# Where the last chunk's residual sum lives, and new offsets and transfer times for the planner that orders a whole transformer block

## The reference, cut to what matters

```python
h = rmsnorm(x, g_mix)
z = h @ w_in                                  # 1024 -> 5120
bc, cc, vc, q, k, va, gc_pre, ga_pre = split(z)
g_c, g_a = sigmoid(gc_pre + b0), sigmoid(ga_pre + b1)
y_c = (bc * causal_dwconv3(cc * vc)) @ w_conv_out
q, k = rope(rmsnorm(q)), rope(rmsnorm(k))     # 4 heads, two sub-heads of 64 each
w = softmax(q0 k0') - lam * softmax(q1 k1')   # lam = exp(..) - exp(..) + lam_init
y_a = (rmsnorm(w @ va) * (1 - lam_init)) @ w_attn_out
x = x + (g_c * y_c + g_a * y_a) @ w_o         # the mix and the residual sum
gt, up = split(rmsnorm(x, g_ffn) @ w_gate_up) # 1024 -> 2 x 2816
x = x + (silu(gt) * up) @ w_down              # 2816 -> 1024
```

## Time and profile before

| | us |
|---|---|
| median of 3 runs (lowest) | 2353.46 (2350.31) |
| the profiled execution | 2351.96 |
| its span, slowest core | 2350.1 |
| spans of its 8 cores | 2330.6 to 2350.1 |
| TensorE busy in that span | 2201.4 (94%) |
| VectorE, ScalarE, GpSimd busy | 1076.7, 1074.0, 478.2 |

### The profile page before, as it was taken

How to read it: one execution, slowest core, us unless ns; L and a number is a source line. 1 busy time by engine, 2 the same in 40 slices (tenths; PEclk the granted TensorE clock), 3 DMA queues, 4 the chain that set the end, 5 groups by cost and what they waited for, 6 DMA issues and landing times.

```text
span 2350.1 us, 45681 instructions; the slowest of 8 cores (2330.6 to 2350.1 us)
## 1 busy us (share of the span) xinstructions
PE 2201.4 (94%) x14976; PEld 1134.7 (48%) x14976; DVE 1076.7 (46%) x2590; ACT 1074.0 (46%) x2011; POOL 478.2 (20%) x797
## 2 busy tenths in 40 slices
PE   5878999999899899999999999999989999999699
PEld 2333454454345444555445554455544555554344
DVE  6875446455443356434554245532435423343432
ACT  4542364363336433466345664456653566641010
POOL 2122335313330124200341003410023200010000
PEclk9998999999999999999999999999999999999899
...
GB/s 198 207 165 162 146 181 161 165 185 182 202 186 193 204 205 167 124 126 169 180 146 128 134 186 140 145 116 136 179 110 144 117 113 141 161 91 175 227 143 175
DMA packets 137031, 376.97 MB, mean 160 GB/s; under 512 B 13536, under 2 KB 34400, under 8 KB 136672
## 3 DMA queue, kind: packets, MB, share of 16 engines
...
## 4 chain that ended last, share of the span: by engine, by line
PE 75%; DMA 12%; issue 5%; DVE 4%; POOL 2%; ACT 2%; SPq 0%; DVEq 0%; POOLq 0%; ACTq 0%
PE bank L788 46%; PE bank L1225 12%; PE bank L1079 10%; PE bank L1053 6%; DMA wP<-wsc 3%; DMA kT<-wblk 2%; DMA xr<-xT 1%; DMA wsc<-wM 1%; DMA xs<-x 1%; DMA wP<-wblk 1%; DMA out<-xr 1%; DMA wM<-wblk 1%; DMA csj<-css 1%; DVE scrM L1148 0%; DMA css<-big 0%
## 5 line engine op out<-in xcount | busy, mean ns | idle before, releaser
L1064 ACT ACTIVATE Pb<-bank 128x512 bf16<-128x512 f32 (+1 forms) x1088 | 557.7, 590 | 271.0 <-PE bank L1053 268.5
L788 PE MATMUL bank<-h,wM 128*128 128x512 bf16 x2720 | 635.7, 383 | 9.1 <-DVE h L1192 8.2
L788 PEld LDWEIGHTS bank<-h,wM 128*128 128x128 bf16 x2720 | 259.0, 98 | 308.8 <-issue 31.4
L788 PE MATMUL bank<-h,wP 128*128 128x512 bf16 x1584 | 380.0, 382 | 11.1 <-DMA wP<-wsc 6.9
L1079 PEld LDWEIGHTS bank<-Vs,Pb 128*128 128x128 bf16 x4224 | 274.8, 99 | 114.6 <-issue 25.8
L1079 PE MATMUL bank<-Vs,Pb 128*128 128x129 bf16 x4224 | 321.8, 221 | 3.3 <-ACT Pb L1064 1.4
L1225 PE MATMUL bank<-big,wM 128*128 128x512 bf16 x1344 | 316.5, 381 | 2.9 <-DMA wM<-wblk 2.9
L788 PEld LDWEIGHTS bank<-h,wP 128*128 128x128 bf16 x1584 | 148.6, 98 | 185.9 <-issue 30.4
L1204 ACT ACTIVATE scrM<-bank 128x512 f32<-128x512 f32 x176 | 105.2, 597 | 287.7 <-PE bank L788 283.9
L1206 DVE SCALAR_TENSOR_TENSOR scrM<-scrM,bank 128x512 f32<-128x512 f32 x176 | 120.6, 685 | 194.6 <-ACT scrM L1204 176.5
L788 PE MATMUL bank<-wP,h 128*128 128x512 bf16 x720 | 175.3, 389 | 21.8 <-DMA wP<-wsc 9.1
...
## 6 DMA issues: line engine op xcount, KB each, us to landing
...
x1s<-big SPq DMA_DIRECT2D x64, 256.0 KB, 5.6
xr<-x1s SPq DMA_DIRECT2D x64, 256.0 KB, 4.5
out<-xr SPq DMA_DIRECT2D x64, 256.0 KB, 3.1
xr<-xT SPq DMA_DIRECT2D x56, 256.0 KB, 4.8
```

The costliest lines, as they stand in the source:

```text
L788: ins = nc.tensor.matmul(out(), lhsT=lhs(k), rhs=rhs(k), start=(k == first), stop=(k == last))
L1064: pl.op("act", lambda P=P, n=n, N=N, s=st[p, n]: nc.scalar.activation(out=Pb[:, P.slot[1], n, 0:N], in_=bk(s)[:, 0:N], func=AF.Exp, scale= ...
```

## The change

Five edits. (1) For the last chunk (j = 7) the residual sum no longer lies in `big`: four of its tiles lie in `h1` and four in the tiles of `scrP`, its `xT` is loaded straight into them, and its AO and WO weights go through `wP` instead of `wM`. A key `x1free` orders these loads behind the eight AO products, which are themselves ordered behind the last reader of `h1`. (2) `PERT` has 24 offsets, one for each stage of each chunk, which shift the priorities of TensorE. (3) Three constants of the model for transfers: those of the first 4 us of the plan are taken as 1.5 times as long and 0.7 us later, and later ones that meet traffic of the other queue as 1.3 us later (`BOTH`). (4) The exponential for `lam` and the two operations behind it wait for the fourth tile of `h1`, not for the first. (5) The scratch tiles of mix 7 have a sequence of their own (`M7`). Edits 2 and 3 change no instruction, only the order.

```diff
-EARLY = 1.0
+EARLY = 1.5
+BOTH = 1300.0
...
-PERT = {}
+PERT = {("A", 0): -0.218, ("A", 1): 0.407, ("A", 2): -0.074, ("A", 3): 0.02, ("A", 4): 0.074, ("A", 5): 0.082, ("A",
+        6): -0.277, ("A", 7): -0.15, ("M", 0): 0.151, ("M", 1): -0.269, ("M", 2): -0.16, ("M", 3): -0.24, ("M", 4): -0.309,
...
+TAILX = True
...
-                b = max(start + DMA_LAT, ring[q])
+                b = max(start + DMA_LAT + (700.0 if start < 4000.0 else 0.0), ring[q])
...
-                fin = ring[q] + 700.0
+                fin = ring[q] + 700.0 + (BOTH if over > 0.0 and start > 4000.0 else 0.0)
...
         def later_trig():
+            pl.op("act", lambda: nc.scalar.activation(out=small[:, SM_E + 2:SM_E + 4], in_=small[:, SM_E:SM_E + 2], func=AF.Exp),
+                  ["sm_e", ("h1", 3)], ["sm_e2"], 200)
...
-        pl.op("act", lambda: nc.scalar.activation(out=small[:, SM_E + 2:SM_E + 4], in_=small[:, SM_E:SM_E + 2], func=AF.Exp),
-              ["sm_e", ("h1", 0)], ["sm_e2"], 200)
...
-            name = "wP" if b < H_AO else "wM"
+            name = "wP" if b < (H_GU if j == NST - 1 and TAILX else H_AO) else "wM"
...
         def mix(j, fp):
+            tail = j == NST - 1 and TAILX
+            spare = [pl.tile("scrP", "P") for _ in range(4)] if tail else []
+
+            def xv(dc):
+
+                if not tail:
+                    return x1[:, dc, :]
+                if dc < 4:
+                    return h1[:, 2 * dc:2 * dc + 2, :].rearrange("p a b -> p (a b)").bitcast(F32)
+                return p_(spare[dc - 4])[:, 0:T]
...
+            free = [("h1", t) for t in range(4)] + ["x1free"] if tail else []
+            need = ["x1free"] if tail else []
...
-                    range(4), 0, 3, lambda part, hh=hh, dc=dc: [hh, ("gateA", dc), ("mixT", dc)] + [("onT", j % NON, k) for k in part], [b], PM)
-                m2 = pl.tile("scrM", "M")
+                    range(4), 0, 3, lambda part, hh=hh, dc=dc: [hh, ("gateA", dc), ("mixT", dc)] + [("onT", j % NON, k) for k in part], [b] + free, PM)
+                m2 = pl.tile("scrM", "M7" if tail else "M")
...
+                if tail:
+                    pl.dma("sp", lambda dc=dc: nc.sync.dma_start(out=xv(dc), in_=xT_d[dc * 128:(dc + 1) * 128, j * T:(j + 1) * T]),
+                           need, xk(dc), ("x0", dc), 262144, 1)
...
-                    out=x1[:, dc, :], in0=bk(b)[:], scalar=0.5, in1=xr[:, xt.slot[1], :] if xt else x1[:, dc, :], op0=ALU.mult, op1=ALU.add),
-                    [b] + ([xt] if xt else x1k(dc)), x1k(dc), DS512)
+                    out=xv(dc), in0=bk(b)[:], scalar=0.5, in1=xr[:, xt.slot[1], :] if xt else xv(dc), op0=ALU.mult, op1=ALU.add),
+                    [b] + need + ([xt] if xt else xk(dc)), xk(dc), DS512)
```

More of the change, by code:

```diff
@@ L1137, in mix, with xk @@
         def mix(j, fp):
+            tail = j == NST - 1 and TAILX
[6 more added lines that the diff above has]
+                return p_(spare[dc - 4])[:, 0:T]
+            def xk(dc):
+                return x1k(dc) if not tail else [("h1x", dc)] if dc < 4 else [spare[dc - 4]]
+            free = [("h1", t) for t in range(4)] + ["x1free"] if tail else []
+            need = ["x1free"] if tail else []
             if j == 0 and X0P:
@@ L1155, in mix @@
                 xt = None
-                if j > 0 or not X0P:
+                if tail:
+                    pl.dma("sp", lambda dc=dc: nc.sync.dma_start(out=xv(dc), in_=xT_d[dc * 128:(dc + 1) * 128, j * T:(j + 1) * T]),
+                           need, xk(dc), ("x0", dc), 262144, 1)
+                elif j > 0 or not X0P:
                     xt = pl.tile("xr", "M")
                     pl.dma("sp", lambda xt=xt, dc=dc: nc.sync.dma_start(
-                        out=xr[:, xt.slot[1], :], in_=xT_d[dc * 128:(dc + 1) * 128, j * T:(j + 1) * T]), [], [xt], ("xr", xt), 262144, 1)
+                        out=xr[:, xt.slot[1], :], in_=xT_d[dc * 128:(dc + 1) * 128, j * T:(j + 1) * T]), need, [xt], ("xr", xt), 262144, 1)
                 b = pl.tile(fp, "M")
@@ L1192, in mix @@
                 pl.op("dve", lambda R=R, dc=dc: nc.vector.scalar_tensor_tensor(
-                    out=h2[:, dc, :], in0=x1[:, dc, :], scalar=cst[:, C_GFFN + dc:C_GFFN + dc + 1], in1=bk(R)[:], op0=ALU.mult,
-                    op1=ALU.mult), x1k(dc) + [R, "cst"], [("h2", dc)], DS512)
+                    out=h2[:, dc, :], in0=xv(dc), scalar=cst[:, C_GFFN + dc:C_GFFN + dc + 1], in1=bk(R)[:], op0=ALU.mult,
+                    op1=ALU.mult), xk(dc) + [R, "cst"], [("h2", dc)], DS512)
         def ffn(j, fp):
```

22 lines of the change are left out of this document (11 added, 11 removed), and 2 rows, old and new, of the table PERT.

## The result

The changed kernel takes 2323.61 us (median of 4 runs, 2313.46 to 2350.89) beside 2351.89 us for the kernel before on the same chip. The ratio is 0.9868, 95% interval 0.9819 to 0.9917. Forecast were 2321 us in a range of 2294 to 2344. One run of each kernel, 2350.89 us of the changed one, was disturbed, and the ratio leaves both out.

The account below looks back on a forecast made before the run. The prediction took TensorE's own work as the bound. Its terms summed as 2351.96 - 19 - 5 + 0 - 8 = 2320 us for the profiled execution, forecast as a 2321 us median, range 2294 to 2344.

Parts of the forecast that it names:

- The last mix: Mix of the last chunk: weaving it with chunk 6's GU removes TensorE's 21.0 us loss, less new waits; -19 us.
- rival (d): Last chunk: the edit does not act, the `x1free` wait costs TensorE 10 us or more; at least 2331 us, chance 0.09.
- The boundary: Where chunk 0 ends: `tabs` operations behind the last head spare it VectorE's wait for `csj`, AO earlier; -5 us.
- The start: First microseconds: moved exponential and new early constants gain nothing, since the weight casts cover it; 0 us, -1.3 to +1.
- The middle: Between 215 and 2189 us: half of the 17.0 us of waits for projection weights goes; -8 us, -25 to +14.
- (b): Rival: the gain stays at the end, only the last mix and the boundary count; 2329 us, chance 0.19.
- (a): Rival: the whole weave improves, the middle giving 25 us and the boundary 9.2; 2299 us, chance 0.24.
- (c): Rival: the changed weave in chunks 4 to 6 is slower, `wP` and `wM` loads holding each other up; 2370 us, chance 0.06.

Follow-up runs that it names:

- tail_m7: tail_plain plus one offset of -0.5 for the last chunk's mix and feed-forward part; 0.9917 of the kernel before.
- tail_plain: Kernel before with only the last chunk's new buffers, its weights through `wP` and the scratch tiles' own sequence, no offsets, old constants; 0.9976 of the kernel before.
- m7_start_exp: tail_m7 with the new constants for the first 4 us and the moved exponential; 0.9886 of the kernel before.
- no_refit: Changed kernel with the old transfer constants, all 24 offsets and the moved exponential kept; 0.9943 of the kernel before.
- exp_back: Changed kernel with the exponential back in its old place, ahead of the first normalised input; 0.9885 of the kernel before.
- no_pert: Changed kernel with only the offset of the last chunk's mix, the 23 others taken out; 0.9863 of the kernel before, 0.9877 when run again.
- np_csj_early: no_pert with chunk 1's eight `tabs` operations moved on VectorE's list ahead of the last steps of chunk 0's last head; 0.9891 of the kernel before.

## Why the prediction was right, and where it wasn't

The forecast was 2321 us, measured were 2323.6 and, by the later ratio, 29.0 us less than before where 32 (1.4%) were forecast. The number came out for the last mix and the boundary, and in part by luck for the rest. By its steps:

**The last mix, -19 (-21 to -13).** Right in size: 19.6 us by tail_m7; taking the buffers out costs 21 to 25, at or beyond the end of the range. The gap-free TensorE from 2100 us on and the clock of 1.00 are as named, but for one wait of 1.42 us, for a load of `wM`, some 80 us behind the `xT` loads. The load of `wM` behind them was costed at nothing. The new waits were taken as 1.5 + 0.5 = 2.0 us and came to 0 and 0.19: the first `xT` load landed in at most 4.3 us, not 7.1, and VectorE stood 1.20 us instead of up to 3.6, behind which TensorE shows no wait. The row used is a median of seven loads, and what counts here is the first of eight. The DMA issues of the changed kernel from 2100 to 2130 us (KB each, median us to landing):

```profile
h<-xT SPq DMA_DIRECT2D x4, 256.0 KB, 5.1
scrP<-xT SPq DMA_DIRECT2D x4, 256.0 KB, 7.0
```

The first four took 5.1 us in the median, the next four 7.0, close to the 7.1 of the earlier trace rows. The rule of the Trainium skill, "DMA: Bandwidth & Descriptors", section "Anatomy of one DMA", which by estimate gives 2.6 us for 256 KB, was too short here (the section gives it for transfers that GpSimd issues, and these are issued by SP), and the row of before too long for the load that counts. By either, TensorE's wait would have been small. The place of the 9.25 us was read rightly and their cause only by half: in tail_plain the waits of VectorE for `xr<-xT` in the midst of WO are gone with the new buffers alone, which gave 5.7 us of whole time; the weave gives the other 13.9. That the edit doesn't act, rival (d), falls: TensorE waited 0 us for the `x1free` chain.

**The boundary, -5 (-9.2 to 0).** Right, in mechanism and size. AO was foretold at about 139.5 and began at 138.5 on the slowest core, and at 138.0 and 140.3 on the means of two executions, from 144.4. The experiments with eight moved operations give 7.3 and 7.6 us at AO, 5.1 and 5.2 a chunk later, and 3.3 to 6.6 in whole times, which the intervals don't tell from 0 by themselves. `csj` was in time behind the head.

**The start, 0 (-1.3 to +1).** Not contradicted for the exponential, open for the constants. Without the exponential ahead the first TensorE instruction comes 1.5 us earlier, and 0.2 of them are left at AO of chunk 0, which one execution of each can't tell from 2. m7_start_exp, which has both start edits, was 7.3 us faster than tail_m7, outside this range if it holds, at the very edge of its interval. And no_refit, with no table load ahead but the old constants, has its first TensorE instruction at 15.3 us, so the constants move it as well. The rule of "ScalarE: Activation LUTs", section "What ACT_TABLE_LOAD costs", in the Trainium skill would have 2.66 us in place of 1.28; here the next activation began 1.29 us after the load did, with no pause ahead of the load either (9.18 us, where the instruction before it ended at 9.16). TensorE's shift of 1.5 us decides nothing between them, since two loads stand ahead in exp_back.

**The middle, -8 (-25 to +14).** Too large, and for the wrong reason. The term was half of the 17.0 us that TensorE waits for `wP<-wsc`. These waits were 17.6 us after the change, where some 8 were foretold. Idle time between 220 and 2100 us fell from 68.4 to 63.6 and 67.6 us on the cores' mean, 1 to 5 us. The whole gain less the other terms leaves 29.0 - 19.6 - 5 = 4 us, by subtraction. The 23 offsets, which were the largest part of the edits it was to come from, are worth 0 within 6 us; no_pert, which did halve these waits (7.7 us), is no faster. What there is came with the constants (tail_m7 to no_pert, 9 to 13 us with the boundary in it). What failed is the step from a wait to a gain: where the waits for these weights fell by 5 to 7 us, the idle time of the middle stayed as it was. My reading, which no run tests further, is that TensorE stands there because it is ahead of its feeders, and earlier loads let it stand somewhere else. Of the rivals, (b), the gain stays at the end and the boundary, 2329, describes the mechanism better than the forecast does; the forecast's number was nearer by luck, because the last mix gave a little more and the rest some us after all, with a cause that the sum didn't name.

**(a), the whole weave improves, and (c), the woven stages cost TensorE.** (a) falls with the middle: 1 to 5 us of idle time are gone there, not 25. Of (c) there is no sign: the idle time from 1050 to 1750 us was 13.7 us before and 15.7 after, that from 1750 to 2100 6.4 and 3.7.

## What to carry to other kernels

Where a stage's norm or sum stands without other work beside it, look first which buffer keeps it from going earlier, and whether the engine that feeds it waits for loads there too: here the buffers were worth 5.7 us by themselves and let one offset win 13.9 more. An operation that reads a late load costs its wait to everything behind it in its engine's list, so eight cheap operations behind the head instead of in it were worth 7 us at the next stage and, a chunk later, 5. And a sum of waits spread over a thousand us is no gain to be halved: 23 offsets moved stages by as much as 62 us and won nothing that could be measured, and neither did halving one queue's waits; take the entries of such a table out again and see whether anything is lost.

## What the runs showed beyond that

The load of `csj`, issued at 117.67 us before and 122.68 after, had landed only at 133.1 before, 15.4 us later, and by 136.9 after; loads of 256 KB at the last mix took 5.1 to 7.1 us in the median. On the slowest cores of four kernels (before, no_refit, np_csj_early, tail_m7) this load kept VectorE for 5.96, 6.19, 6.59 and 8.37 us. Between cores of one execution AO of chunk 0 begins up to 6.0 us apart in the kernel before, so a step of 5 us near the start isn't read from one core: the mean of eight gave 7.3 and 7.6 us for the same edit in both directions, and even that mean differed by 3.0 us between executions with the same lists up to there.
